# A ring of three weight slabs in the memory of two, split two slabs ahead of TensorE

## What is computed

```python
# first block
h = rms_norm(x, g_mix); z = h @ w_in                      # 1024 -> 3136
a = mla(c_q, c_kv, k_r, ...)                              # latent attention, 4 heads
r = hgrn2(hq, hf_f, hf_b, hi, hg, ...)                    # gated linear attention, both directions
x = x + concat([a, r]) @ w_o
x = x + (silu(h @ w_gate) * (h @ w_up)) @ w_down          # h = rms_norm(x, g_ffn), 1024 -> 2816 -> 1024
x = x + sigmoid(rms_norm(x, g_ple) @ w_ple_gate) * (p @ w_ple_proj)
# second block
proj = rmsnorm(x) @ w_in_2                                # 1024 -> 8192: q, k, v, g, u, sv, a_ret, a_sgu
y_ret = retention(q, k, v, g); y_sgu = spatial gating(u, sv)
merged = sigmoid(a_ret) * y_ret + sigmoid(a_sgu) * y_sgu
x = x + rmsnorm(merged @ w_out)
x = x + rmsnorm((gelu(a) * b) @ w_down_2)                 # a, b = depthwise conv of h2 @ w_up_2
```

## Time and profile before

| | us |
|---|---|
| median of 3 runs | 1839.24 |
| lowest, highest | 1838.3, 1842.51 |
| profiled execution, its own time | 1844.86 |
| span of its profile | 1843.6 |
| TensorE matmul busy | 1703.0 (92%) |
| TensorE weight load busy | 1383.5 (75%) |
| VectorE busy | 908.5 (49%) |
| ScalarE busy | 621.1 (34%) |

### The profile page before, as it was taken

How to read it: one execution, slowest core, us unless ns; L and a number is a source line. 1 busy time by engine, 2 the same in 40 slices (tenths; PEclk the granted TensorE clock), 3 DMA queues, 4 the chain that set the end, 5 groups by cost and what they waited for, 6 DMA issues and landing times.

```text
span 1843.6 us, 18637 instructions
## 1 busy us (share of the span) xinstructions
PE 1703.0 (92%) x7861; PEld 1383.5 (75%) x7861; DVE 908.5 (49%) x1189; ACT 621.1 (34%) x761; POOL 11.2 (1%) x24
## 2 busy tenths in 40 slices
PE   6998968889999999999898989999998799999995
PEld 5787735557788887877787779878877588887884
DVE  5434467655444442136753643345343776676214
ACT  4324334433323221125542333223333444444111
POOL 1000000000000000000000000000000000000000
PEclk9998958899999999999899999999999799999997
DMA  5322100002332233232231122222322122232211
GB/s 156 93 70 69 46 29 1 1 24 69 108 98 91 92 110 107 92 109 69 69 98 50 44 73 92 92 69 91 108 75 91 46 92 92 93 112 93 92 68 46
DMA packets 122178, 143.75 MB, mean 78 GB/s; under 512 B 5993, under 2 KB 113856, under 8 KB 122096
## 3 DMA queue, kind: packets, MB, share of 16 engines
q1 hardware_dynamic: 120816, 139.87, 23.5%
q0 software_dynamic: 1088, 2.64, 0.5%
q10 hardware_dynamic: 192, 0.07, 0.0%
HBM read 140.46 MB, written 2.10 MB: 77 GB/s over the span
## 4 chain that ended last, share of the span: by engine, by line
PE 88%; DVE 7%; ACT 3%; issue 2%; DMA 1%; SPq 0%; DVEq 0%; ACTq 0%
PE bank L336 26%; PE bank L338 26%; PE bank L337 26%; PE bank L374 2%; PE bank L523 1%; PE bank L707 1%; PE bank L569 1%; DVE tmp L820 1%; PE bank L509 1%; PE bank L508 1%; PE bank L564 1%; PE bank L690 1%; PE bank L532 1%; DVE slab_lo L807 1%; DMA x_tm<-in_x 0%
## 5 line engine op out<-in xcount | busy, mean ns | idle before, releaser
L336 PE MATMUL bank<-h_hi,slab_hi 128*128 128x512 f32 x1384 | 552.9, 399 | 28.2 <-DVE h_lo L812 16.8
L337 PE MATMUL bank<-h_lo,slab_hi 128*128 128x512 f32 x1384 | 546.2, 395 | 0.0
L338 PE MATMUL bank<-h_hi,slab_lo 128*128 128x512 f32 x1384 | 546.0, 394 | 0.0
L807 DVE TENSOR_TENSOR slab_lo<-slab_raw,slab_hi 128x2048 fp32r<-128x2048 f32 x130 | 297.9, 2292 | 378.3 <-ACT slab_hi L1471 378.1
L1471 ACT ACTIVATE slab_hi<-slab_raw 128x2048 fp32r<-128x2048 f32 x130 | 247.9, 1907 | 268.8 <-PE bank L338 264.9
L336 PEld LDWEIGHTS bank<-h_hi,slab_hi 128*128 128x128 f32 x1384 | 264.8, 191 | 91.7 <-issue 29.9
L337 PEld LDWEIGHTS bank<-h_lo,slab_hi 128*128 128x128 f32 x1384 | 264.9, 191 | 57.6 <-issue 2.5
L338 PEld LDWEIGHTS bank<-h_hi,slab_lo 128*128 128x128 f32 x1384 | 264.0, 191 | 55.8
L336 PE MATMUL bank<-hid_hi,slab_hi 128*128 128x512 f32 x352 | 139.3, 396 | 1.7 <-issue 1.7
L337 PE MATMUL bank<-hid_lo,slab_hi 128*128 128x512 f32 x352 | 139.2, 395 | 0.0
L338 PE MATMUL bank<-hid_hi,slab_lo 128*128 128x512 f32 x352 | 139.2, 395 | 0.0
(11 more groups left out here) (345 smaller groups left out, 1705.3 us busy)
## 6 DMA issues: line engine op xcount, KB each, us to landing
slab_raw<-in_w_in SPq DMA_DIRECT2D x40, 1024.0 KB, 5.1
slab_raw<-in_w_up SPq DMA_DIRECT2D x33, 1024.0 KB, 5.1
slab_raw<-in_w_down SPq DMA_DIRECT2D x22, 1024.0 KB, 4.9
slab_raw<-in_w_gate SPq DMA_DIRECT2D x11, 1024.0 KB, 5.3
slab_raw<-in_w_o SPq DMA_DIRECT2D x4, 1024.0 KB, 5.2
slab_raw<-in_w_ple_gate SPq DMA_DIRECT2D x4, 1024.0 KB, 5.1
slab_raw<-in_w_ret_o SPq DMA_DIRECT2D x4, 1024.0 KB, 5.1
slab_raw<-in_w_sgu_o SPq DMA_DIRECT2D x4, 1024.0 KB, 5.0
```

What stands on the lines that cost most here:

```text
L336: T.matmul(ps, a_hi, b_hi, start=start, stop=False, skip_group_check=skip)
L337: T.matmul(ps, a_hi, b_lo, start=False, stop=False, skip_group_check=skip)
L338: return T.matmul(ps, a_lo, b_hi, start=False, stop=stop, skip_group_check=skip)
L807: V.tensor_tensor(w_lo[g % 2][:, :], raw[g % 2][:, :], w_hi[g % 2][:, :].bitcast(F32), ALU.subtract).then_inc(slab_lo, 1)
```

## The change

`raw`, `w_hi` and `w_lo` get three buffers each, and `w_lo[j]` is at the address of `raw[j]`: the lo part is written over the slab, so that the three tensors take as much memory as before. The buffers are used by g % 3. Since a raw buffer is now in use until TensorE has ended its slab, SyncE issues the load of slab g after TensorE's end of slab g - 3. `split(g)` is called at the same places, but does slab g + 1 (at g = 0 slabs 0 and 1), so that each slab is split one place earlier in the programs; ScalarE waits for TensorE's end of slab (g + 1) - 3 before it. The two split instructions cover only the columns that the slab fills.

```diff
+RING = 3
...
-    raw = [sb(f"slab_raw{j}", [P, SLAB]) for j in range(2)]
-    w_hi = [sb(f"slab_hi{j}", [P, SLAB], F32R) for j in range(2)]
-    w_lo = [sb(f"slab_lo{j}", [P, SLAB], F32R) for j in range(2)]
+
+    raw_at = [top[0] + j * SLAB * 4 for j in range(RING)]
+    raw = [sb(f"slab_raw{j}", [P, SLAB]) for j in range(RING)]
+    w_lo = [sb(f"slab_lo{j}", [P, SLAB], F32R, at=raw_at[j]) for j in range(RING)]
+    w_hi = [sb(f"slab_hi{j}", [P, SLAB], F32R) for j in range(RING)]
...
-    landed_at = [16 * sum(len(slabs[k][1]) for k in range(g % 2, g + 1, 2)) for g in range(len(slabs))]
+    slab_size = [columns * srcs[0].shape[1] for columns, srcs in slabs]
+    landed_at = [16 * sum(len(slabs[k][1]) for k in range(g % RING, g + 1, RING)) for g in range(len(slabs))]
...
# VectorE
+        def split_one(g):
+            V.wait_ge(slab_hi, g + 1)
+            j, n = g % RING, slab_size[g]
+            V.tensor_tensor(w_lo[j][:, 0:n], raw[j][:, 0:n], w_hi[j][:, 0:n].bitcast(F32),
+                            ALU.subtract).then_inc(slab_lo, 1)
+
         def split(g):
-            V.wait_ge(slab_hi, g + 1)
-            V.tensor_tensor(w_lo[g % 2][:, :], raw[g % 2][:, :], w_hi[g % 2][:, :].bitcast(F32),
-                            ALU.subtract).then_inc(slab_lo, 1)
+
+            if g == 0:
+                split_one(0)
+            if g + 1 < len(slabs):
+                split_one(g + 1)
...
# ScalarE
+        def split_one(g):
+            j, n = g % RING, slab_size[g]
+            A.wait_ge(slab_landed[j], landed_at[g])
+            if g >= RING:
+                A.wait_ge(psum_ready, slab_end[g - RING])
+            A.activation(w_hi[j][:, 0:n], raw[j][:, 0:n], ACT.Copy).then_inc(slab_hi, 1)
+
         def split(g):
-            A.wait_ge(slab_landed[g % 2], landed_at[g])
-            if g >= 2:
-                A.wait_ge(psum_ready, slab_end[g - 2])
-            A.activation(w_hi[g % 2][:, :], raw[g % 2][:, :], ACT.Copy).then_inc(slab_hi, 1)
+
+            if g == 0:
+                split_one(0)
+            if g + 1 < len(slabs):
+                split_one(g + 1)
...
# SyncE
         for g, (columns, srcs) in enumerate(slabs):
-            if g >= 2:
-                SP.wait_ge(slab_lo, g - 1)
+            if g >= RING:
+                SP.wait_ge(psum_ready, slab_end[g - RING])
```

More of the change, by code:

```diff
@@ L216, in program @@
     bank_read = [sem(f"bank_read{b}") for b in range(8)]
-    slab_landed = [sem(f"slab_landed{j}") for j in range(2)]
+    slab_landed = [sem(f"slab_landed{j}") for j in range(RING)]
     slab_hi, slab_lo = sem("slab_hi_done"), sem("slab_lo_done")
@@ L342, in slab_fm @@
             T.wait_ge(slab_lo, g + 1)
-            hv, lv = (w[g % 2][:, :].rearrange("p (k c) -> p k c", k=KT) for w in (w_hi, w_lo))
+            hv, lv = (w[g % RING][:, :].rearrange("p (k c) -> p k c", k=KT) for w in (w_hi, w_lo))
             ps = [take(names[t], 2 * (g % 2) + t) for t in range(2)]
@@ L408, in tensor_program @@
         T.wait_ge(slab_lo, 3)
-        hv, lv = (w[0][:, 0:KT * P].rearrange("p (k c) -> p k c", k=KT) for w in (w_hi, w_lo))
+        hv, lv = (w[2 % RING][:, 0:KT * P].rearrange("p (k c) -> p k c", k=KT) for w in (w_hi, w_lo))
         ps = take("kr", 0)
@@ L453, in tensor_program @@
         T.wait_ge(slab_lo, 11)
-        hv, lv = (w[0][:, 0:2 * HEADS * QK].rearrange("p (k c) -> p k c", k=2) for w in (w_hi, w_lo))
+        hv, lv = (w[10 % RING][:, 0:2 * HEADS * QK].rearrange("p (k c) -> p k c", k=2) for w in (w_hi, w_lo))
         T.wait_ge(c_lo_done, 2)
@@ L466, in tensor_program @@
         T.wait_ge(slab_lo, 13)
-        hv, lv = (w[0][:, :].rearrange("p (k h c) -> p k h c", k=2, h=HEADS) for w in (w_hi, w_lo))
+        hv, lv = (w[12 % RING][:, :].rearrange("p (k h c) -> p k h c", k=2, h=HEADS) for w in (w_hi, w_lo))
         T.wait_ge(c_lo_done, 4)
@@ L622, in down @@
                 T.wait_ge(slab_lo, g + 1)
-                hv, lv = (w[g % 2][:, :].rearrange("p (k c) -> p k c", k=2) for w in (w_hi, w_lo))
+                hv, lv = (w[g % RING][:, :].rearrange("p (k c) -> p k c", k=2) for w in (w_hi, w_lo))
                 T.wait_ge(lo_done, 2 * s + 2)
@@ L645, in tensor_program @@
         T.wait_ge(slab_lo, PLE + 1)
-        hv, lv = (w[PLE % 2][:, :].rearrange("p (k c) -> p k c", k=2) for w in (w_hi, w_lo))
+        hv, lv = (w[PLE % RING][:, :].rearrange("p (k c) -> p k c", k=2) for w in (w_hi, w_lo))
         for k in range(2):
@@ L1933, in sync_program @@
         for g, (columns, srcs) in enumerate(slabs):
-            if g >= 2:
-                SP.wait_ge(slab_lo, g - 1)
+            if g >= RING:
+                SP.wait_ge(psum_ready, slab_end[g - RING])
             k = srcs[0].shape[1]
-            dst = raw[g % 2][:, 0:k * columns].rearrange("p (k c) -> p k c", k=k)
+            dst = raw[g % RING][:, 0:k * columns].rearrange("p (k c) -> p k c", k=k)
             at = 0
@@ L1940, in sync_program @@
                 n = int(np.prod(src.shape[2:]))
-                SP.dma_start(dst[:, :, at:at + n] if len(srcs) > 1 else dst, src).then_inc(slab_landed[g % 2], 16)
+                SP.dma_start(dst[:, :, at:at + n] if len(srcs) > 1 else dst, src).then_inc(slab_landed[g % RING], 16)
                 at += n
```

## The result

The changed kernel takes 1858.0 us (median of 4 runs, 1851.8 to 1867.7), the kernel before 1839.0 (4 runs, 1838.3 to 1842.5): ratio 1.0094, 95% interval 1.0064 to 1.0123. It is slower by 0.9%, 3.5 us beyond the forecast's 1854.5 and inside its range. The profiled execution took 1860.4 us.

The account below looks back on a forecast made before the run. TensorE, busy 92% of the span, was taken to bound the kernel, with time lost at seams. Terms 1 to 8 summed to 13.2 us, plus 2 for the clock: 15.2 on 1839.24 gave 1854.5 us, range 1845 to 1864.

Parts of the forecast that it names:

- The steady stage: Within stages: hi starts at E + 5.1, lo ends at E + 9.45, then tile 0; no loss, E being TensorE's slab end.
- rival B: Inside FF and UP2: blocked splits also stall TensorE, +11 to 22 us beside the 15, 1870 us; chance 0.06.
- A: Rival: loads do not block, as engines reach splits later than E + 5 at seams; 1839.3 or 1837 us; chance 0.08.
- C: Rival at the norms: earlier splits leave VectorE free for the sum of squares, a gain, 1832 us; chance 0.04.
- up to 5 us times some 100: Sign: growth of VectorE's idle time before its half of the split (L807).
- Term 1: Start: slab 1 split before the first norm_tile, so TensorE's first slab starts at 23.9 instead of 21.67; +2.2 us.
- Term 2: Latent normalization: hi, squares, lo, kr's scaling and sums come later behind the load; +4.2 us.
- Term 3: k tiles: hi after slab 11 and everything behind move by 4.35, 1.1 us of it slack; +3.25 us.
- Terms 4 to 7: Seams: FF to DOWN +1.15, DOWN to PLE +2.0, PLE to IN2 +1.05, BR2 to WOUT +1.1, BR1 +0.4 us.
- Term 8: Second v slab: split before the decay tables, so TensorE's wait of 2.16 us goes; -2.15 us.
- Edits costed at 0: Smaller splits of slabs 2 and 10, hidden by TensorE's slabs, and the in-place subtract (at most 0.1 us on lo): 0.
- Term 9, the clock: Four pauses made or lengthened (terms 2, 3, 5, 7) may drop TensorE to its lower clock; +2 us, bounds 0 to 8.

Follow-up runs that it names:

- e1: Changed kernel with each split call splitting its own slab, one ahead of TensorE; three buffers, lo over raw and late load kept: 1835.6 us.
- e2: e1 with the ring cut from three buffers to two: 1860.4 us.
- e5: Changed kernel with the start alone undone, slab 1 split at its old place behind the first norm's sums: 1854.1 us.
- e3: Changed kernel with two splits moved behind the norm work at the latents and the k tiles, on VectorE and ScalarE: 1848.3 us.
- e4: Changed kernel with each single-DMA load issued as two halves one after the other, some 2.3 us longer: 1879.4 us.
- e6: Kernel before with only the narrow splits of slabs 2 and 10 added: 1834.6 us, ratio 0.9936 to 0.9975.
- e8: e7 without its move of UP2's first split, so e1 with three splits moved: 1831.6 us, ratio 0.9938.
- e7: e1 with four splits moved to places where their engine idles (second v slab, UP2, slab 10, slab 15): 1834.6 us.

## Why the prediction was right

The steady stage came out as written: in the z stage hi 5.3 us after the slab's end (111.22; E is 105.9), lo ending at E + 9.5, tile 0 right behind it, tile 1 at E + 10.9. Nothing stalled inside a stage: the shift between the two kernels' matmuls is 14.7 us at 315 us of the changed kernel and still 14.7 at the end of FF, and no pause within UP2 grew, so rival B is out. A falls by its own deciding point, the hi copy's releaser, and by e1 and e2; C falls with the norms, where h_lo and the sums of squares are waited for longer (21.1 and 20.3 us in place of 16.8 and 16.2), not shorter. VectorE's idle time before the split grew by 215 us; the "up to 5 us times some 100" was a bound and far above.

- Term 1: 2.2 for 2.2, first slab at 23.73 for 23.9. e5 takes away just this.
- Term 2: 4.1 for 4.2; the wait of 5.56 was forecast as 5.7. Term 3: 3.7 for 3.25. The forecast let only ScalarE's hi move. The row that binds is one behind: 

```profile
197.01 1.91 ACT L1484 ACTIVATE slab_hi<-slab_raw 128x2048 fp32r<-128x2048 f32 x1 [4.53 <-DMA slab_raw<-in_w_in]
201.89 1.23 ACT L1575 ACTIVATE tmp<-k_nope 128x512 f32<-128x512 f32 x2 [2.96 <-DVE k_nope L863]
```

ScalarE's square waits for VectorE's copy, and the copy for lo. The distance from hi to the square, 4.88, is that of the earlier trace rows (4.87), so the order was right; most of the 0.4 us is in when hi came: slab 11 ended at 191.6, its load took 5.3 us and hi started 5.4 after the end, not 5.1. e3 confirms both terms.
- Terms 4 to 7: 1.1, 2.4, 1.7, and 1.1 and 1.3, for 1.15, 2.0, 1.05, and 0.4 and 1.1: 7.6 for 5.7. The mechanism is that of e4's dose. (In term 4 the working has 694.0 where 691.4 + 2.75 is 694.15.) DOWN's end is the plainest, VectorE, beside the earlier trace rows:

```profile
829.05 2.29 DVE L812 TENSOR_TENSOR slab_lo<-slab_raw,slab_hi 128x2048 fp32r<-128x2048 f32 x1 [9.31 <-ACT slab_hi L1484]
831.26 4.86 DVE L1135 TENSOR_TENSOR residual<-residual,bank 128x512 f32<-128x512 f32 x8
836.82 0.69 DVE L1174 TENSOR_TENSOR p_lo<-bank,p_hi 128x512 fp32r<-128x512 f32 x1 [0.70 <-ACT p_hi L1722]
```

  All eight adds stand behind lo, as worked out. What was too small is the load. I took the median, 5.1 us; at these seams the load took, from issue to landing, 5.1 (FF to DOWN), 5.4 (DOWN to PLE), 5.8 (PLE to IN2), 5.9 (BR1) and 5.0 (WOUT). The terms missed by -0.1, 0.4, 0.7, 0.7 and 0.2: all but WOUT's 0.2 goes with the load.
- Term 8: -2.3 for -2.15.
- Edits costed at 0: the subtract over its operand, right (e1). The narrow splits, right in idle time of TensorE (0.6) and wrong in time: e6 shows them worth some 7 us in the kernel before.
- Term 9, the clock, is the term that was mis-sized: 2 forecast, with bounds 0 to 8. The medians lie 19.0 apart and the pauses give 13.1, so 5.9 are left, or 4.6 with the pauses at 14.4; both are in the bounds. Low clock beside the new pauses is there (TensorE behind the k tiles, two 4 us windows, next-to-last fields PEclk, DMA share, GB/s):

```profile
204.00:208.00 4.00, 4.00 (x15) 3.42 (x14) 0.69 (x1) 0.03 (x1) 0.00 (x0) 0.50 0.00 0
...
216.00:220.00 4.00, 4.00 (x13) 3.42 (x14) 2.37 (x5) 0.78 (x2) 0.00 (x0) 0.50 0.00 0
```

  It is not one price per pause. The 18 us at 0.50 from 202.6 us on cost 8.0 us of shift, and later as much came back: the matmuls that the kernel before ran between 270 and 294 us, mostly at the lower clock, ran at full speed in the changed one, and the shift fell from 22.4 to 14.6.
- Luck: that the idle time grew by 13.1 us for a sum of 13.2 is in part chance. The terms came to 15.3, and 1.3 at the first transposes and 1.2 at k_rope, which are in no term, took 2.5 of them off.

## What to carry to other kernels

A ring buys time only for what is started before it is due: with lo over raw the third buffer moved the split forward and the load with it, so each split waited out the whole transfer. In an in-order queue that wait is paid by whatever stands behind it; look for it at the seams, where TensorE has nothing else, and place the waiting instruction behind the seam's own work (e3) or where its load has long landed (e1, e8). A load's median is also not what a seam pays: it was 5.1 us, and 5.0 to 5.9 at the seams. A change in several parts should be taken apart even when its sum is a loss: one part of this one, two splits made narrower, was a gain by itself.

## What the runs showed of the hardware

TensorE's clock moves the time of this kernel by up to 12 us and is not a function of TensorE's program. In one session runs of the kernel before went from 1836.9 us at a mean granted clock of 0.955 to 1848.8 at 0.948; those of the changed kernel from 1851.8 at 0.951 to 1867.7 at 0.941. The kernel before, and then e6, in the same window, in nearly the same place of the same TensorE program (e6 came out of the wait for kr 1.4 us later):

```profile
156.00:158.00 2.00, 2.00 (x7) 1.71 (x8) 0.00 (x0) 0.44 (x1) 0.00 (x0) 0.50 0.00 0
```

```profile
156.00:158.00 2.00, 2.00 (x14) 1.82 (x13) 0.69 (x1) 0.63 (x1) 0.00 (x0) 1.00 0.51 174
```

Seven matmuls beside fourteen, both with TensorE busy for the whole window. The kernel before stood at the lower level from 154 to 168 us although TensorE had worked without a pause since 144.5; e6 and e1 stood at full speed there. They differ by 0.8 us in the wait for kr ahead of it. But the length of that wait is not the rule: in e7 it was 3.3 us, and TensorE stood at the lower clock from 151 to 168; in e8 3.4, and it stood there from 152 to 162. What tips it stays open.
